# Six places for split weight halves in an expert trunk kernel, instead of four

## The reference, cut to what matters

```python
for l in range(DEPTH):                                   # DEPTH = 2, 256 tokens, width D = 2048, all float32
    proj = rms_norm(x, attn_norm[l]) @ w_in[l]           # (2048, 6149): q, k, v of 16 heads of three kinds
    mixed = concat(diff_attention, stick_breaking_attention, forgetting_attention)
    x = x + mixed @ w_out[l]
    x = x + moe_ffn(rms_norm(x, ffn_norm[l]), ...)

def moe_ffn(h, ...):                                     # 16 experts, two chosen for each token
    hg = einsum('nd,edf->nef', t, wg)                    # wg, wu: (16, 2048, 512)
    hu = einsum('nd,edf->nef', t, wu)
    act = silu(hg) * hu * combine
    out = einsum('nef,efd->nd', act, wd)                 # wd: (16, 512, 2048)
```

## Time and profile before

| | |
|---|---|
| median of 3 runs | 2081.04 us (2078.16 to 2086.06) |
| profiled execution | 2096.89 us, of which the span is 2095.2 us |
| busy in the span | PE 1914.3 us (91%), DVE 1600.9 (76%), ACT 1437.7 (69%), POOL 91.1 (4%) |
| chain that ended last | PE 64%, issue 11%, ACT 11%, DVE 10%, DMA 4% |
| loads of expert units | 384 of 1024 KB each, 8.8 us from issue to landing (median) |

### The profile page before, as it was taken

One profiled execution on the slowest core, in us unless ns is written; L12 is line 12 of the kernel. 1 busy time (PEld: TensorE's weight loads), 2 busy tenths in 40 slices (PEclk: granted clock), 3 DMA queues, 4 the chain that ended last, 5 costly groups with the idle time before them and its releaser, 6 DMA issues.

```text
span 2095.2 us, 31139 instructions
## 1 busy us (share of the span) xinstructions
PE 1914.3 (91%) x9018; PEld 1502.2 (72%) x9018; DVE 1600.9 (76%) x2274; ACT 1437.7 (69%) x2276; POOL 91.1 (4%) x86
## 2 busy tenths in 40 slices
PE   6999999995999999999889999999959999999997
PEld 5877777884777777767668777778847777767775
DVE  4567667545999999999855676675469999999997
ACT  4455665442889889898654656654438889898895
POOL 0000000000001000000000000000010001000000
PEclk9999999995999999999899999999969999999998
DMA  8434444553899999999764343445549999999995
GB/s 322 160 137 146 157 144 141 181 221 127 336 403 398 404 399 401 409 391 421 309 230 158 141 161 141 141 147 180 215 158 383 403 409 399 407 395 394 405 416 222
DMA packets 82864, 582.12 MB, mean 278 GB/s; under 512 B 11662, under 2 KB 11918, under 8 KB 13166
## 3 DMA queue, kind: packets, MB, share of 16 engines
q1 hardware_dynamic: 75600, 542.01, 66.8%
q0 software_dynamic: 7168, 38.94, 5.3%
HBM read 575.91 MB, written 29.36 MB: 289 GB/s over the span
## 4 chain that ended last, share of the span: by engine, by line
PE 64%; issue 11%; ACT 11%; DVE 10%; DMA 4%; ACTq 0%; DVEq 0%; SPq 0%; POOL 0%; POOLq 0%
PE bank L817 9%; PE bank L819 9%; PE bank L818 9%; PE bank L986 6%; ACT wh L554 6%; PE bank L970 6%; PE bank L988 5%; PE bank L987 5%; PE bank L972 5%; DVE wl L1156 4%; PE bank L953 2%; DMA proj<-in_expert_units 1%; ACT rows L751 1%; PE bank L961 1%; ACT wide L655 1%
## 5 line engine op out<-in xcount | busy, mean ns | idle before, releaser
L1156 DVE TENSOR_TENSOR wl<-raw,wh 128x1024 fp32r<-128x1024 f32 x640 | 766.6, 1222 | 333.2 <-ACT wh L554 332.1
L554 ACT ACTIVATE wh<-raw 128x1024 fp32r<-128x1024 f32 x640 | 664.3, 1055 | 424.0 <-PE bank L819 343.0
L1156 DVE TENSOR_TENSOR wl<-proj,wh 128x1024 fp32r<-128x1024 f32 x384 | 455.0, 1221 | 41.2 <-ACT wh L554 40.8
L970 PE MATMUL bank<-wh,xh 128*128 128x512 f32 x1024 | 430.4, 420 | 33.5 <-DVE wl L1156 30.5
L554 ACT ACTIVATE wh<-proj 128x1024 fp32r<-128x1024 f32 x384 | 395.0, 1053 | 74.6 <-PE bank L988 52.2
L817 PE MATMUL bank<-wh,xh 128*128 128x512 f32 x1024 | 420.1, 410 | 12.1 <-DVE wl L1156 8.3
L972 PE MATMUL bank<-wl,xh 128*128 128x512 f32 x1024 | 408.3, 399 | 0.0
L819 PE MATMUL bank<-wh,xl 128*128 128x512 f32 x1024 | 405.1, 396 | 0.0
L818 PE MATMUL bank<-wl,xh 128*128 128x512 f32 x1024 | 404.1, 395 | 0.0
L970 PEld LDWEIGHTS bank<-wh,xh 128*128 128x128 f32 x1024 | 195.7, 191 | 121.0 <-DVE wl L1156 81.0
L817 PEld LDWEIGHTS bank<-wh,xh 128*128 128x128 f32 x1024 | 196.1, 191 | 58.3 <-DVE wl L1156 13.8
(11 more groups left out here) (228 smaller groups left out, 1575.0 us busy)
## 6 DMA issues: line engine op xcount, KB each, us to landing
raw<-in_expert_units SPq DMA_DIRECT2D x192, 1024.0 KB, 8.8
proj<-in_expert_units SPq DMA_DIRECT2D x192, 1024.0 KB, 8.8
raw<-in_in_units SPq DMA_DIRECT2D x96, 1024.0 KB, 4.8
raw<-in_out_units SPq DMA_DIRECT2D x32, 1024.0 KB, 4.8
expert_rows<-rows POOLq DMA_DIRECT2D x4, 1024.0 KB, 4.1
proj<-picks POOLq DMA_DIRECT2D x4, 1024.0 KB, 6.9
x<-in_x SPq DMA_DIRECT2D x2, 1024.0 KB, 6.7
wide<-in_norms POOLq DMA_DIRECT2D x2, 1024.0 KB, 5.0
```

Of the source, the lines that this page charges most:

```text
L554: act_(wh[:, h % CUT, :], ring[j][:, h % 2 * HALF:(h % 2 + 1) * HALF], ACT.Copy)\
L970: mm(bank[m][:, :], stacked[b][:, 2 * h + c, :], wh[:, j, k], start=(h + c == 0), stop=False)
L1156: v.tensor_tensor(wl[:, h % CUT, :], ring[(first + h // 2) % slots][:, h % 2 * HALF:(h % 2 + 1) * HALF], wh[:, h % CUT, :].bitcast(F32), A ...
```

## The change

There are six places for split halves in the expert stage. `high` and `low` are lists: four places are those of `wh` and `wl`, and two more pairs lie in `xl`, the buffer of the rows' low parts, which the expert stage doesn't use otherwise but for the table `back`. That table moves to `qkT` in two pieces. The dense stage keeps `cut` and four places. TensorE raises `cut_free` by 2 more at the start of an expert stage, and ScalarE takes them back at its end. `part_slot` picks the place. All that stood behind cut h now stands behind cut h + 2 on ScalarE and VectorE (in the first step the sigmoid and the silu of the gate are put closer to the copy, since there are only 16 halves). On TensorE the order of the halves is as before; only the transposes of the next expert's tokens (`XT`) come one half earlier.

```diff
+DEEP_CUT = 6
-XT = {False: {PART + 4: 0, 2 * PART + 1: 1}, True: {2: 0, PART + 2: 1}}
-XT_MOVE = {f: {h + CUT + 1: g for h, g in at.items()} for f, at in XT.items()}
+XT = {False: {PART + 3: 0, 2 * PART: 1}, True: {2: 0, PART: 1}}
+XT_MOVE = {f: {h + DEEP_CUT + 1: g for h, g in at.items()} for f, at in XT.items()}
-GATE_OUT = {first: at + CUT for first, at in GATED_AT.items()}
+GATE_OUT = {first: at + DEEP_CUT for first, at in GATED_AT.items()}
-UP_OUT = CUT - 1
+UP_OUT = DEEP_CUT - 1
-STORE = {PLAN[False].rindex("d") + CUT - 3 * PART + k: n for n, k in enumerate((0, 1, 3, 5))}
+STORE = {PLAN[False].rindex("d") + DEEP_CUT - 3 * PART + k: n for n, k in enumerate((0, 1, 3, 5))}
+def part_slot(h, first=False):
+    return (h if first else h + 2 * PART) % DEEP_CUT
...
-        back = xl[:, 0, :]
+        back = [table(192, P), table(852, P)]
+        spare_cut = xl[:, :, :].rearrange("p (k c) n -> p k (c n)", k=4)
+        high = [wh[:, j, :] for j in range(CUT)] + [spare_cut[:, j, :] for j in range(2)]
+        low = [wl[:, j, :] for j in range(CUT)] + [spare_cut[:, 2 + j, :] for j in range(2)]
...
+            def part_cut(h, at, first=False):
+                j = (at + h // 2) % DEEP
+                if h % 2 == 0:
+                    e.wait_ge(S[f"raw_landed{j}"], t_.due(f"raw_landed{j}", 16))
+                e.wait_ge(S["cut_free"], t_.due("cut_free"))
+                act_(high[part_slot(h, first)], ring[j][:, h % 2 * HALF:(h % 2 + 1) * HALF], ACT.Copy)\
+                    .then_inc(S["hi_ready"], 1)
...
-                        cut(h, DEEP, at)
-                        if h == CUT - 1 and first:
+                        part_cut(h, at, first)
+                        if h == DEEP_CUT - 1 and first:
...
                 with t_.one_round():
+                    e.sem_inc(S["cut_free"], DEEP_CUT - CUT)
```

More of the change, by code:

```diff
@@ L792, in _ @@
                     for h in range(PART):
-                        cut(h, DEEP, 4)
-                        if h == 1 or h == 2:
-                            store(0, h - 1, NE - 2)
+                        part_cut(h, 4)
+                        if h in (UP_OUT - 2, UP_OUT - 1):
+                            store(0, h - UP_OUT + 2, NE - 2)
                         if h == UP_OUT:
@@ L969, in up_half @@
                     k = slice(c * COLS, (c + 1) * COLS)
-                    mm(bank[m][:, :], stacked[b][:, 2 * h + c, :], wh[:, j, k], start=(h + c == 0),
+                    mm(bank[m][:, :], stacked[b][:, 2 * h + c, :], high[j][:, k], start=(h + c == 0),
                        stop=False)
-                    last = mm(bank[m][:, :], stacked[b][:, 2 * h + c, :], wl[:, j, k], start=False,
+                    last = mm(bank[m][:, :], stacked[b][:, 2 * h + c, :], low[j][:, k], start=False,
                               stop=(h == PART - 1 and c == 1))
@@ L985, in down_half @@
                     o = bank[2 + 2 * (h % 2) + c][:, :]
-                    mm(o, actT[:, k, 0:STACK], wh[:, j, r], start=(k == 0), stop=False)
-                    mm(o, actT[:, k, 0:STACK], wl[:, j, r], start=False, stop=False)
-                    last = mm(o, actT[:, k, SLOTS:SLOTS + STACK], wh[:, j, r], start=False, stop=(k == 3))
+                    mm(o, actT[:, k, 0:STACK], high[j][:, r], start=(k == 0), stop=False)
+                    mm(o, actT[:, k, 0:STACK], low[j][:, r], start=False, stop=False)
+                    last = mm(o, actT[:, k, SLOTS:SLOTS + STACK], high[j][:, r], start=False, stop=(k == 3))
                 last.then_inc(S["cut_free"], 1)
@@ L1015, in join @@
                     for t in range(NT):
-                        last = mm(bank[JOIN_BANK[j] + t][:, :], back[:, t * P:(t + 1) * P].bitcast(F32),
+                        last = mm(bank[JOIN_BANK[j] + t][:, :], back[t],
                                   rows[:, 0, j * COLS:(j + 1) * COLS], start=True, stop=True)
@@ L1023, in step @@
                     if part == "d":
-                        down_half(n, h % CUT)
+                        down_half(n, part_slot(h, first))
                     else:
-                        up_half(b, "gu".index(part), n, h % CUT)
+                        up_half(b, "gu".index(part), n, part_slot(h, first))
                     if first and h in LISTED:
@@ L1158, in cut, with part_cut @@
                                 wh[:, h % CUT, :].bitcast(F32), ALU.subtract).then_inc(S["lo_ready"], 1)
+            def part_cut(h, at, first=False):
+                j = part_slot(h, first)
+                e.wait_ge(S["hi_ready"], t_.due("hi_ready"))
+                v.tensor_tensor(low[j], ring[(at + h // 2) % DEEP][:, h % 2 * HALF:(h % 2 + 1) * HALF],
+                                high[j].bitcast(F32), ALU.subtract).then_inc(S["lo_ready"], 1)
             def inverse_root(st, a, b, scale, to=None):
@@ L1629, in last_tables @@
                 def last_tables():
-                    v.tensor_copy(back, bank[4][:, P:P + SEQ])
+                    for t in range(NT):
+                        v.tensor_copy(back[t], bank[4][:, (1 + t) * P:(2 + t) * P])
                     v.tensor_copy(last_weight[SLOTS:STACK, :], bank[4][SLOTS:STACK, 4 * NE:4 * NE + 4])
@@ L1687, in step @@
                             act_lo()
-                        if h == GATE_OUT[first] + 4:
+                        if h == GATE_SILU[first]:
                             gate_silu()
```

11 lines of the change are left out of this document (7 added, 4 removed).

## The result

| | before | after |
|---|---|---|
| median | 2088.53 us (15 runs, 2078.16 to 2098.78) | 2075.73 us (15 runs, 2062.28 to 2086.13) |
| profiled execution | 2096.89 us, span 2095.2 | 2080.62 us, span 2078.8 |

The ratio is 0.9938, with a 95% interval of 0.9916 to 0.9960. The change makes the kernel faster by 0.6%, some 13 us (by the interval 8 to 18). My 2065 was 10.7 us too low, and the time lies 0.7 us above the range that I gave (2040 to 2075).

The account below looks back on a forecast made before the run. Engines with four places and the DMA (share 1.01) were taken to run at nearly the same pace, the DMA with no idle time left. Tail gains 8.3 + 7.5 = 15.8 us off 2081.0 gave 2065, range 2040 to 2075.

Parts of the forecast that it names:

- The first rival: Whole kernel: engines set the pace and the DMA follows; 2037 at 415 GB/s, 2024 with DMA out of the way; chance 0.2.
- my term of nothing for the steady state: Expert steps: waits for TensorE turn into waits for landings, gain nothing; bound for the range 14 us a layer.
- The tails: End of each layer's expert stage: 8.3 us less in the first layer, 7.5 us less in the second.
- Six cuts ahead of `add_picks(0)`: Tails: halves 0 to 5 ready before the picks' additions, only 6 and 7 behind; first layer's 3.98 us TensorE stall goes.
- My sum: Both layers together: 8.3 + 7.5 = 15.8 us off the profiled span, 0.75%.
- The second rival: Only the first tail's stall of 3.98 us and its clock go, about 3 us: 2074; chance 0.22.
- `up_out` two cuts later: Tails: stands behind the third unit's cuts, yet starts 2.5 us earlier in the first layer, 7.3 us in the second.
- The slower rival: Every expert step: longer idle time at TensorE's fold lowers the clock, 60 us lost, 2141; chance 0.08.
- The start: Start of each expert stage: two cuts in VectorE's idle time put the DMA one unit ahead; last landing 2.6 us earlier.
- The second layer: Second expert stage's tail: ends 7.5 us earlier, with the engines 7 us behind the data before the change.
- X: Landing of a stage's last unit: 1025.3 to 1022.7 in the first layer, 2058.5 to 2055.9 in the second.
- The base: Whole kernel: the 15.8 us were taken off a median of 2081.0, which gave 2065.

Follow-up runs that it names:

- the first experiment: The changed kernel with VectorE's gated, act_lo and add_picks(0) put back behind cut 3 in the tail; ratio to the kernel before 0.9986, median 2084.21 us.

## Why the prediction was right and wrong

**What bounds the kernel: right.** The two experiments with half the bytes show the engines' two paces side by side: 32.38 us with four places, and 30.58 us with six. I had put the engines' floor at 30.75. That the DMA would take this gain, as its share of 1.01 and the growing time to landing said, is shown by the 62 us between those two kernels and the 13 us between the full ones. The first rival, at 2037 or 2024, fell. Its price at 415 GB/s was never paid either, since the long stretches ran at 405 and 406. But that is a little above 403, so my term of nothing for the steady state was too small: by the estimate above some 2.6 us a layer.

**The tails: right in kind, and they carry the gain.** Six cuts ahead of `add_picks(0)` are worth 0.48% by the first experiment (0.9986 against 0.9938), 10 us of 13. My sum has about 6 for it, all in the first layer: without it the second layer's tail would stop too (3.16 us in the row above), since the engines are no longer behind the data there. In the first layer the last stores begin 1049.34 - 1038.45 = 10.9 us earlier, and the stage's first matmul 2.15 us (504.48 and 502.33 in the two timelines): 8.7 us in the stage, where I had 8.3. What lies behind the last landing came out as forecast: my ends, 1041.0 and 2074.3, stand 17.7 and 17.8 us behind the picks' issues that I forecast (1023.3 and 2056.5), and 18.2 and 17.8 us were measured. The second rival, a stall's worth only, was right in part, and the gain ended between it (2074 of 2081, 0.34%) and my forecast (0.77%).

**`up_out` two cuts later: right in place, dearer than priced.** It waits for the third unit, and TensorE idles 3.40 us before the fold, where it was 2.83. In the steps between 560 and 1000 there are 14 such waits of 29.3 us together, the longest 4.6, where they were 16.9 and 1.2. The slower rival's mechanism is there: the clock is at 0.98, not 1.00. A cost of it isn't seen, since the DMA's rate did not fall. That the DMA's backlog covers it is argued.

**The start: not shown.** I gave it 2.6 us in each layer. The bytes in the start rose from 153 to 197 GB/s, but with the tail's order put back, start and catch-up together are worth 0.14% with an interval from 0.34% to nothing. In the first layer, where both profiled executions began at half clock, the picks' issue moved from 521.4 to 518.0 us behind the first matmul. That is 3.4 us, and in keeping with the term, but it is one pair of executions, and the higher rate of the steady state is in it too.

**The second layer: the last landing, the term that was mis-sized.** I had 7.5 us from the engines' lag of 7.3 us behind the data. In the two profiled executions the last stores move by 15.9 us (from 2081.99 to 2066.11), but the first matmul had already moved by 15.1 (from 1548.56 to 1533.46), so 0.8 us lie in the stage. The part behind the landing is as forecast. The landing isn't: "X is 2058.5 there and becomes 2055.9" puts the picks' issue 507.9 us behind the stage's first matmul, and it came at 514.8, where it had been at 510.5. Both executions differ in something that the change doesn't touch. In the kernel before the clock was up 3 us after the stage began, and in the changed one only after 20 us:

```profile
1551.00:1572.00 21.00, 18.99 (x129) 14.76 (x128) 15.63 (x26) 13.49 (x15) 1.33 (x2) 0.91 0.54 184
```

```profile
1536.00:1554.00 18.00, 18.00 (x90) 14.11 (x90) 6.58 (x14) 5.48 (x7) 0.24 (x1) 0.50 0.34 119
```

I took what one execution did, which had started at full clock, for a property of the kernel. The profiles of the kernels with full loads and no idle matmuls bear this out. In eight of their stages the clock is at 0.50 for the first 20 us, and the picks' issue stands 514.8 to 521.4 us behind the first matmul. In three it is up after some 3 us (0.93 over the 20 us), and it stands at 509.2 to 510.5. In the other three the clock rises and falls again (0.59), and it stands at 511.9 to 515.7. The kernel before and the changed one are each in both of the first two groups. That the clock alone makes the difference isn't shown, since no run held it fixed.

That the profiled time was forecast well, 2081.1 us against 2080.62, is luck. Of the 16.4 us between the two spans, 2.2 lie ahead of the first expert stage and 15.1 - 10.9 = 4.2 in the second dense stage. The change touches neither. They make up for the 6.7 us that the second expert stage lacks.

**The base: the step that put the time out of the range.** "The same off the median of 2081.0 gives 2065": the three runs shown had a median of 2081.04, fifteen had 2088.53, and later sets of twelve and more 2086.5 to 2088.7. This is 7.5 of the 10.7 us. Of the other 3.2 us 3.0 are the sum's, 15.8 us against 12.8, and the rest is rounding. As a ratio my forecast was 0.9923, inside the measured interval, so by the runs' times the sum isn't shown to be wrong. I had compared the sum with the profiled 2096.9 us and read the 15.9 us between it and the median as something that the profiler might do. It isn't: the changed kernel's profiled 2080.62 us lies inside its own runs, and the kernel before reaches 2098.78 without it. Single executions spread over 20 us here. A base taken from one profile and three runs carries that spread, and my range had left no room for it.

## What to carry to other kernels

When the busiest engines and the DMA run at nearly the same pace, a wait list names only one of them. Read the DMA's share and how its time to landing grows along the stage, before pricing a wait that more buffers would remove. More places then pay where the DMA isn't the bound: at the end of a stage, where they let matmuls go on past an in-order wait of another engine. Halving the bytes, in the kernel before and in the changed one, shows what the deeper pipeline could give. And before a term is read from one execution, look at a second one of the same kernel: here a stage's last landing differed by 8.8 us between two of them, more than any term of my sum.

## What the runs showed that I had not expected

The granted clock can stay at half for some 20 us while TensorE works without a gap. At the start of the first expert stage of the changed kernel it is 0.50 for 21 us with 21.00 us busy:

```profile
503.00:524.00 21.00, 21.00 (x98) 16.48 (x97) 8.60 (x20) 6.83 (x7) 0.93 (x1) 0.50 0.34 121
```

It does so again after it was at full a few microseconds before, in the run with idle matmuls (0.50 and 0.51 from 503 to 515 above). What TensorE has to do doesn't tell which: the same stretch of the same kernel stood at 0.93 in its other execution (505 to 526 above). At which moment the clock rises differs from execution to execution (3 us or 20 us into the same stage), and with it, in the traces here, goes a shift of 4 to 9 us in that stage's last landing. How much of the 20 us of spread between runs comes from it I can't say, since only a few of them have a trace.
